# Attention outputs computed with v stationary, two heads on TensorE's two column halves, in a fused four-layer block

## What is computed

```python
# per head, 64 wide; 16 heads in a and b, 8 in h; k and v are shared by groups of heads
s = q @ k.T * scale + mask            # 256 x 256, causal: three 128x128 tiles are computed
p = exp(s - max)                      # in a, the sink joins the maximum and the denominator
o = (p @ v) / (p.sum(-1) [+ exp(sink - max)])
o = o * silu(z)                       # in a and b only: the gate
h = h + concat(o) @ w_out
# h: every key counts mult = [d<=128] + [d%4==0] + [d%16==0] times (three dilated patterns)
```

## Time and profile before

| | |
|---|---|
| median of 3 runs | 895.84 us (895.56 to 895.88) |
| the profiled execution | 895.39 us, its span 893.6 us |
| granted TensorE clock | 0.998 of full speed |
| TensorE matmul | 881.1 us busy (99%), 4570 instructions |
| TensorE weight loads | 725.3 us (81%) |
| VectorE | 557.4 us (62%) |
| ScalarE | 515.0 us (58%) |
| GpSimd | 132.6 us (15%) |
| DMA | 146.36 MB, 164 GB/s on average |

### The profile page before, as it was taken

How to read it: one execution, slowest core, us unless ns; L and a number is a source line. 1 busy time by engine, 2 the same in 40 slices (tenths; PEclk the granted TensorE clock), 3 DMA queues, 4 the chain that set the end, 5 groups by cost and what they waited for, 6 DMA issues and landing times. The chain is left out here.

```text
span 893.6 us, 12331 instructions
## 1 busy us (share of the span) xinstructions
PE 881.1 (99%) x4570; PEld 725.3 (81%) x4570; DVE 557.4 (62%) x982; ACT 515.0 (58%) x849; POOL 132.6 (15%) x104
## 2 busy tenths in 40 slices
PE   8999999999999999999999999999999999999996
PEld 5888887888878878888888887888878888888885
DVE  5855876548766677755555446566677755555444
ACT  5677566774768765644444334768765644444332
POOL 0122144121053430000000000143420000000001
PEclk9999999999999999999999999999999999999999
DMA  8732454425443334665555555544335665555521
GB/s 294 285 100 82 164 192 142 142 95 161 167 160 113 135 115 149 209 216 182 181 180 185 191 188 182 170 142 141 101 136 154 207 205 189 187 186 182 192 101 47
DMA packets 94750, 146.36 MB, mean 164 GB/s; under 512 B 6500, under 2 KB 54884, under 8 KB 94692
## 3 DMA queue, kind: packets, MB, share of 16 engines
q1 hardware_dynamic: 92804, 139.52, 46.8%
q0 software_dynamic: 1296, 4.72, 1.6%
q10 hardware_dynamic: 592, 1.34, 0.5%
HBM read 144.52 MB, written 1.05 MB: 163 GB/s over the span
## 5 line engine op out<-in xcount | busy, mean ns | idle before, releaser
L985 DVE TENSOR_TENSOR lo<-raw,hi 128x1024 fp32r<-128x1024 f32 (+1 forms) x244 | 301.3, 1260 | 132.5 <-ACT hi L1284 130.4
L1284 ACT ACTIVATE hi<-raw 128x1024 fp32r<-128x1024 f32 (+1 forms) x260 | 266.7, 1056 | 79.2 <-PE bank L1125 77.1
L1125 PE MATMUL bank<-hi,xT_hi 128*128 128x512 f32 (+2 forms) x736 | 291.8, 397 | 2.3 <-DVE xT_lo L1732 0.7
L1125 PE MATMUL bank<-hi,xT_lo 128*128 128x512 f32 (+2 forms) x736 | 283.0, 385 | 0.0
L1125 PE MATMUL bank<-lo,xT_hi 128*128 128x512 f32 (+2 forms) x736 | 282.1, 383 | 0.0
L1125 PEld LDWEIGHTS bank<-hi,xT_hi 128*128 128x128 f32 x736 | 138.4, 188 | 35.7 <-issue 8.7
L1125 PEld LDWEIGHTS bank<-hi,xT_lo 128*128 128x128 f32 x736 | 138.2, 188 | 28.2
L1125 PEld LDWEIGHTS bank<-lo,xT_hi 128*128 128x128 f32 x736 | 138.6, 188 | 24.8 <-issue 0.5
L1125 PE MATMUL bank<-hi,hT 128*128 128x512 f32 x352 | 111.5, 395 | 0.0
L1125 PEld LDWEIGHTS bank<-hi,hT 128*128 128x128 f32 x352 | 66.3, 188 | 15.4
L1125 PE MATMUL bank<-lo,hT 128*128 128x512 f32 x176 | 69.4, 394 | 0.0
(11 more groups left out here) (243 smaller groups left out, 1027.6 us busy)
## 6 DMA issues: line engine op xcount, KB each, us to landing
raw<-in_w_in SPq DMA_DIRECT2D x26, 1024.0 KB, 5.0
raw<-in_w_gate SPq DMA_DIRECT2D x44, 512.0 KB, 3.7
raw<-in_w_up SPq DMA_DIRECT2D x44, 512.0 KB, 4.7
raw<-in_w_down SPq DMA_DIRECT2D x22, 1024.0 KB, 4.8
raw<-in_w_out SPq DMA_DIRECT2D x20, 1024.0 KB, 5.0
raw<-in_w_in_b SPq DMA_DIRECT2D x10, 1024.0 KB, 5.1
raw<-in_w_in_a SPq DMA_DIRECT2D x8, 1024.0 KB, 7.1
raw<-in_w_in_a SPq DMA_DIRECT2D x4, 256.0 KB, 5.1
```

Source lines behind the costliest of these rows:

```text
L985: return engine.tensor_tensor(lo[r][:, cols], raw[c.i % RAW][:, cols], hi[r][:, cols].bitcast(F32), ALU.subtract)
L1125: last = nc.tensor.matmul(bank[:, 0:wd], still[a], mv[r][:, off:off + wd], start=c.first and i == 0 and j == 0, stop=c.last and i == len(t ...
L1284: nc.scalar.activation(hi[c.i % SPLIT][:, cols], raw[c.i % RAW][:, cols], ACT.Copy)\
```

## The change

- `v1` becomes `v`, 64 wide, without ones. In `pv`, v is stationary and probT moves: head 0 of the pair goes to the lower 64 columns of the array and of PSUM, head 1 to the upper 64, both into one bank, with 256 and then 128 moving columns for each. The outputs come out transposed, `o` is now [128, pairs, 256].
- The flips' copies to probT are all by VectorE. One pv step now handles both heads and signals once. A copy of a flip waits for the pv of the pair before it.
- In a round the order becomes: flips of pair n-1, pv of pair n-2, scores of pair n. The banks are asked for as F0, F1, V, S0, S1.
- The exponentials write their sums beside (`accum_out`) to `totals`, and `den` takes these. In h, `mult` moves into the exponent: `log_mult`, in float32, is added where the mask was.
- `gate` is now one GpSimd operation (silu(z) times reciprocals, or in h a copy of the reciprocals). It, not the output, is transposed (`turn_gate`); VectorE multiplies the bank with `o` in place, and `split_o` splits `o` into hi (ScalarE) and lo (VectorE) of oT. The gates of the second half are filled before the output product instead of after its first half chunk.

The core of the diff:

```diff
@@ attention(sc, n)
-    if 2 <= n <= pairs + 1:
-        a["obank"] = sc.bank()
-        for head in (2 * n - 4, 2 * n - 3):
-            s = sc.step("pv", head=head, att=a, bank=a["obank"], p=a["base"] + head)
-            a["pv"].append(s)
-        by_vector = (n == 4) if a["kind"] != "h" else n in (3, 5)
-        o = sc.step("vector_oev" if by_vector else "oev", att=a, pair=head // 2, bank=a["obank"], pv=s)
     if 1 <= n <= pairs:
         for head in (2 * n - 2, 2 * n - 1):
             b = sc.bank()
-            s = sc.step("flip", head=head, att=a, bank=b, p=a["base"] + head,
-                        n=len(a["flip"]) + (sc.mult_flips if a["kind"] == "h" else sc.plain_flips))
-            b.freed = (s, "vector" if a["kind"] == "h" else "scalar")
+            s = sc.step("flip", head=head, att=a, bank=b, p=a["base"] + head)
+            b.freed = (s, "vector")
             a["flip"].append(s)
+    if 2 <= n <= pairs + 1:
+        b = sc.bank()
+        s = sc.step("pv", pair=n - 2, att=a, bank=b, p=a["base"] + 2 * n - 4)
+        o = sc.step("oev", att=a, pair=n - 2, bank=b, pv=s)
+        b.freed = (o, "scalar")
@@ turn_gates(sc, a, half, *ms)
     for m in ms or range(M):
-        sc.oturned[half, m] = sc.turn(a["gates"][half][m], "o", 4 * half, m)
+        b = sc.bank()
+        s = sc.step("turn_gate", att=a, half=half, m=m, of=a["gates"][half][m], oev=a["oev"][4 * half + 3], bank=b)
+        b.freed = (s, "vector")
+        sc.turned_quarter(s)
+        sc.oturned[half, m] = sc.step("split_o", att=a, half=half, m=m, of=s)
@@ mixer_ab
+    fill_gates(sc, a, 1, zb)
     out_product(sc, w_out, KD, {
-        0: (att(9), [lambda: fill_gates(sc, a, 1, zb)]),
+        0: (att(9), ()),
@@ TensorE, pv
+                ended(pe, a["flip"][2 * s.pair + 1], "vector")
+                bank, v = freed(pe, s.bank), B["v"]
+                for r in range(2):
+                    nc.tensor.matmul(bank[64 * r:64 * r + 64, 0:S], v[:, 0, kv, :], B[f"probT{r}"][:, 0:S],
+                                     start=True, stop=False)
+                for r in range(2):
+                    last = nc.tensor.matmul(bank[64 * r:64 * r + 64, P:S], v[:, 1, kv, :], B[f"probT{r}"][:, S:QC],
+                                            start=False, stop=True)
+                last.then_inc(sem["pv", "tensor"], 1)
@@ ScalarE, scores
-                nc.scalar.activation(pr[:, 0:P], bank[:, 0:P], ACT.Exp, scale=-1.0, bias=shift[:, hd, 0:1])
+                nc.scalar.activation(pr[:, 0:P], bank[:, 0:P], ACT.Exp, scale=-1.0, bias=shift[:, hd, 0:1],
+                                     accum_out=totals[:, hd, 0:1])
                 done(nc.scalar.activation(pr[:, P:QC], bank[:, P:QC], ACT.Exp, scale=-1.0,
-                                          bias=shift[:, hd, 1:2]), s)
+                                          bias=shift[:, hd, 1:2], accum_out=totals[:, hd, 1:2]), s)
@@ VectorE
-            elif s.kind == "flip" and s.att["kind"] == "h":
+            elif s.kind == "flip":
                 dve.wait_ge(sem["flip", "tensor"], s.i + 1)
                 if s.i >= 2:
-                    dve.wait_ge(sem["pv", "tensor"], s.i - 1)
-                done(tt(Hb[f"probT{s.p % 2}"][:, :], psum[4 + s.bank.at][:, 0:QC], mult, ALU.mult), s)
+                    dve.wait_ge(sem["pv", "tensor"], s.i // 2)
+                done(nc.vector.tensor_copy(B[f"probT{s.p % 2}"][:, :], psum[4 + s.bank.at][:, 0:QC]), s)
+            elif s.kind == "turn_gate":
+                dve.wait_ge(sem["turn_gate", "tensor"], s.i + 1)
+                ended(dve, s.oev, "scalar")
+                o = B["o"][:, 4 * s.half:4 * s.half + 4, s.m * P:(s.m + 1) * P]
+                done(tt(o, psum[4 + s.bank.at][:, :].rearrange("p (k t) -> p k t", k=4), o, ALU.mult), s)
+            elif s.kind == "split_o":
+                ended(dve, s, "scalar")
+                done(tt(oT[1][:, ks, ms], B["o"][:, ks, ms], oT[0][:, ks, ms].bitcast(F32), ALU.subtract), s)
```

More of the change, by code:

```diff
@@ L431, in fill_gates @@
     es = a["sinks"][half] if a["kind"] == "a" else None
-    den = sc.step("den", att=a, half=half, es=es, oev=a["oev"][4 * half + 3])
-    a["gates"][half] = [sc.quarter("gate" if half and not m else "pool_gate", att=a, half=half, m=m, z=z, den=den) for m in range(M)]
+    den = sc.step("den", att=a, half=half, es=es)
+    a["gates"][half] = [sc.quarter("gate", att=a, half=half, m=m, z=z, den=den) for m in range(M)]
 def turn_gates(sc, a, half, *ms):
     for m in ms or range(M):
-        sc.oturned[half, m] = sc.turn(a["gates"][half][m], "o", 4 * half, m)
+        b = sc.bank()
[3 more added lines that the diff above has]
+        sc.oturned[half, m] = sc.step("split_o", att=a, half=half, m=m, of=s)
 def new_attention(sc, which, heads, nkv):
-    if sc.heads:
-        count_flips(sc)
-    a = sc.att = {"kind": which, "heads": heads, "nkv": nkv, "scores": [], "flip": [], "pv": [], "oev": [],
+    a = sc.att = {"kind": which, "heads": heads, "nkv": nkv, "scores": [], "flip": [], "oev": [],
                   "base": sc.heads, "tk": [], "tq": [], "gates": {}, "sinks": []}
@@ L956, in freed @@
             step, who = bank.before.freed
-            if step.kind == "flip":
-                eng.wait_ge(sem["flip", who], step.n + 1)
-            else:
-                ended(eng, step, who)
+            ended(eng, step, who)
         return psum[4 + bank.at]
@@ L1191, in _ @@
             elif s.kind == "pv":
[L1192 removed]
+                a = s.att
                 B = Hb if a["kind"] == "h" else A
[L1194 to L1203 removed]
+                kv = 2 * s.pair // (a["heads"] // a["nkv"])
+                ended(pe, a["flip"][2 * s.pair + 1], "vector")
[8 more added lines that the diff above has]
+            elif s.kind == "turn_gate":
+                ended(pe, s.of, "gpsimd")
+                bank = freed(pe, s.bank)
+                for i in range(4):
+                    last = transpose(bank[:, i * P:(i + 1) * P], quarter[s.of.buf][:, i * P:(i + 1) * P])
+                last.then_inc(sem["turn_gate", "tensor"], 1)
             elif s.kind == "sums":
@@ L1439, in _ @@
                 ended(act, s.pv, "tensor")
-                W1 = HD + 1
-                src = psum[4 + s.bank.at][:, 0:4 * W1].rearrange("p (g m d) -> p m g d", g=2, m=2)
-                done(nc.scalar.activation(B["o"][:, :, 2 * s.pair:2 * s.pair + 2, :], src, ACT.Copy), s)
+                done(nc.scalar.activation(B["o"][:, s.pair, :], psum[4 + s.bank.at][:, 0:S], ACT.Copy), s)
+            elif s.kind == "split_o":
+                B = Hb if s.att["kind"] == "h" else A
+                ended(act, s.of, "vector")
+                ks, ms = slice(4 * s.half, 4 * s.half + 4), slice(s.m * P, (s.m + 1) * P)
+                done(nc.scalar.activation(oT[0][:, ks, ms], B["o"][:, ks, ms], ACT.Copy), s)
             elif s.kind == "sink":
@@ L1564, in _ @@
                 last.then_inc(sem["pool_rope", "gpsimd"], 1)
-            if s.kind == "pool_gate":
-                B = Hb if s.att["kind"] == "h" else A
+            if s.kind == "gate":
                 if s.before is not None:
@@ L1821, in _ @@
                 done(tt(esink[:, e, :], shift[:, e, :], spread(sinks[:, 0, e].unsqueeze(2), [P, 8, M]), ALU.add), s)
-            elif s.kind == "vector_oev":
-                B = Hb if s.att["kind"] == "h" else A
-                ended(dve, s.pv, "tensor")
-                W1 = HD + 1
-                src = psum[4 + s.bank.at][:, 0:4 * W1].rearrange("p (g m d) -> p m g d", g=2, m=2)
-                done(nc.vector.tensor_copy(B["o"][:, :, 2 * s.pair:2 * s.pair + 2, :], src), s)
             elif s.kind == "den":
-                B = Hb if s.att["kind"] == "h" else A
-                ended(dve, s.oev, PARTS[s.oev.kind][0])
-                d = B["o"][:, :, 8 * s.half:8 * s.half + 8, HD]
+                ended(dve, s.att["scores"][8 * s.half + 7], "scalar")
@@ L1832, in _ @@
+                d = totals[:, 8 * s.half:8 * s.half + 8, :]
                 if s.es is not None:
                     ended(dve, s.es, "scalar")
-                    e = esink[:, 8 * s.half:8 * s.half + 8, :].rearrange("p s m -> p m s")
-                    chained(tt(dens[:, :, :], d, e, ALU.add))
+                    chained(tt(dens[:, :, :], d, esink[:, 8 * s.half:8 * s.half + 8, :], ALU.add))
                     d = dens[:, :, :]
                 done(nc.vector.reciprocal(dens[:, :, :], d), s)
-            elif s.kind == "gate":
+            elif s.kind == "turn_gate":
```

105 lines of the change are left out of this document (37 added, 68 removed).

## The result

| | before | after |
|---|---|---|
| median | 895.83 us (895.36 to 895.88) | 914.52 us (913.77 to 914.91) |
| ratio | | 1.0209, 95% interval 1.0194 to 1.0224 |
| span of the profiled execution | 893.6 us | 912.9 us |

The account below looks back on a forecast made before the run. TensorE, issuing without a gap, was taken to bound the kernel. Each mixer loses 2.7 + 4.0 + 1.5 - 0.2 = 8.0, two 16.0, hybrids 0: 895.4 + 16.0 = 911.4 profiled, so 911.8 median; range 903 to 921.

Parts of the forecast that it names:

- pv 0.8 from its first matmul: pv of a head pair on TensorE's column halves: 0.8 us instead of 1.29, between bounds of 0.72 and 1.4.
- The ring: Four PSUM banks: scores wait for VectorE's copy of F0, itself behind pv; TensorE's shortest round becomes 6.0 us.
- The chain through the splits: Plain rounds: exponentials, hi split, lo split, copy, scores in series set a period of 6.50 us against 5.77.
- Round 2: Mixers a and b: flips' copies delay VectorE's maxima, so scores end at 54.7 instead of 51.95, a loss of 2.7.
- The output product's start: After round 7 of a mixer: VectorE's multiplication now precedes the hi and lo splits; a loss of 1.5 us.
- Mixer a's second half of the output product: Second gates filled earlier get a half chunk more time; TensorE waits for none of it, cost 0.
- Hybrid rounds: Hybrid layers: rounds 2 and 3 lose 0.35 each, rounds 4 and 5 gain 0.4 each; together nothing.
- What costs nothing: VectorE's 32 new copies, GpSimd's single gate, earlier second gates, memset, mask transfer, read-outs in h: TensorE waits for none.
- The clock, rival at 0.03: TensorE's clock falls in gaps of 0.5 to 2.5 us; a few half chunks make 920 and more; chance 0.03.
- The second rival: Only pv, copy, scores in series binds: rounds 4 to 7 take 6.0 each, total 906.2 us; chance 0.17.
- The third: Rival: pv's two column halves don't run together, so pv costs 1.4 and the total is 919.8 us; chance 0.15.
- the first: Rival: F0's copy is in time and TensorE keeps its pace, 24 pairs gain 0.43, total 888.5 us; chance 0.08.

Follow-up runs that it names:

- the padded one: The changed kernel with 640 unused bytes a partition ahead of hT, so hT lies where the kernel before has it; 918.61 us, ratio 1.0260.

## Why the prediction was right, point by point

- **That TensorE bounds and any delay of it lengthens the kernel** held: span less busy time grew from 12.5 to 37.5 us while TensorE's own work fell by 6, and the earlier trace rows has become a list.
- **pv 0.8 from its first matmul:** 0.80 from start to start where the flips follow it, 0.87 to the end of its last instructions, and 1.5 to that end for one half after the other. Between the bounds of 0.72 and 1.4, as placed.
- **The ring**, scores behind F0's copy behind pv: 12 and 4 waits, 17.4 us, at the line named. The two kernels with other bank or step orders moved the wait to ScalarE's copy and brought plain rounds to 5.9 and 5.4.
- **The chain through the splits, 6.5 a plain round:** 6.33. The term that was too large is the read-outs' 0.4. From the first exponential to the hi split it is 1.61 now (82.15 to 83.76) and was 1.30, so 0.31 for four; the hi split starts at 2.54 and not at 2.67, and the copy follows 0.2 earlier than worked out. Without read-outs a round gains only 0.16, as the series, 6.17 where 6.0 was worked out, binds then. Over rounds 3 to 7 of a the loss is 3.4 instead of 4.0.
- **Round 2, 2.7:** 2.0. The way was right, one size was off: round 1's lo split, which stands ahead of the copies and the maxima, took 1.55 and not the 1.86 of the earlier trace rows (it starts 0.3 later beside GpSimd's rope; that this is the reason is not shown), and the read-outs took less. That copies ahead of the maxima make most of it was shown by giving them to ScalarE: 0.4 left with all of them moved, and 0.9 gained in each second round with only round 1's two moved, in the kernel with pv first.
- **The output product's start, 1.5:** 1.3 in a and 1.2 in b. The sum itself was loose: its three handoffs went in with 0.15 together, and by the text's own 0.1 each the term is 1.65. The way was partly another. pv of pair 6 got the bank that the first gate's multiplication held and waited 1.1 (the third line of the waits), which the text had not listed. Round 9 gained 0.35, predicted 0.2.
- **Mixer a's second half of the output product, 0:** 1.6. The edit that fills the second gates earlier was costed at nothing; VectorE's multiplication and lo come behind three lo splits beside GpSimd's gates, and the second tile's oT lo is 1.0 late. In b nothing is lost: the same three splits begin 1.6 us ahead of the half chunk's start that they stand beside (214.43 against 216.03), in a 0.1 behind it (101.20 against 101.08), and only a has the sinks' exponential ahead of them. No run tests that this is the reason. "I use a's values for b, whose list is the same" was wrong here: b has no sinks.
- **Hybrid rounds, 0:** 0.3 and 0.2, with 0.6 and 0.4 lost in rounds 2 and 3 and 0.3 and 0.4 gained in 4 and 5.
- **"What costs nothing" was the wrong step.** It listed copies, gates, memset and read-outs, but not the new shape of turning and splitting: a chain of six operations over two engines in strict order. It costs 4.8 us in the two scans besides the clock, and grouping four steps took all but 0.8 of it away. The earlier trace rows had the terms (0.59 and 0.68 each), and the output product's start was worked out with them; the same sum was not made for the hybrid layers, where ScalarE's next work was what counted.
- **The clock, rival at 0.03:** it was no alternative but an addition, 2.3 us in the profiled execution, and with a mean granted clock of 0.992 to 0.995 none of the five executions was free of it. That it would take "gaps, each of 0.5 to 2.5" was right; "a few half chunks, 920 and more" was not.
- **The addresses, not thought of:** -2.7. With the clock's 2.3 it nearly cancels, so the range would have been met without either.

The second rival, only the series pv, copy, scores binds, 906.2, was near: a round of 6.17 without read-outs against 6.33. The third is excluded by 0.87, the first by the waits.

The Trainium skill's "TensorEngine Tiling (Array Packing)", PSUM Bottleneck, says that once tiling has sped TensorE up, the copies out of PSUM may become the bottleneck. Its direction agrees: what the scores wait for is such a copy. But the copy's own 0.5 us is not the limit: with the flips' copies still on VectorE, another order, and a few of the output copies handed back to VectorE, 897.2 was reached.

## What to carry to other kernels

When steps are reordered, redo the ring of buffers by hand: who gets whose bank, who frees it, and what stands ahead of that on the freeing engine, in every round that differs and not only in the plain one. When one operation on each of two tiles becomes a chain across two in-order engines, issue it stage by stage and not tile by tile, and ask what the engine does next. And before a gain of 0.3% is credited to a change, put the large buffers at equal addresses in both kernels.

## What the runs showed of the hardware

- A shift of 640 bytes a partition in SBUF of the operand that 528 matmuls read changes each from 395 to 390 ns and the kernel by 2.9 us, with the same instructions and their other operand (hi, lo) where it was. The Trainium skill ("SBUF — State Buffer", SBUF: two separate sides) says, of contention between engines, that TensorE never waits on anyone. No run here shows whether the 5 ns are a wait; they come with the address of hT, and no run shows by which rule.
- TensorE's granted clock fell to its 1.2 GHz level behind gaps of 1.8 to 2.2 us at the scores, and also behind waits of 0.9 and 0.5 among short matmuls. It fell at different places in kernels with almost the same gaps (the changed kernel at 660 us, the padded one not; the kernel with pv first behind its waits in round 4, not behind those of 2 us in the hybrids), and cost 1.6 and 2.3 us where it could be set apart. So the gain of closing a gap can be more than the gap, and varies.
- A sum read out behind an exponential takes 0.19 to 0.21 us in the timeline, but four of them moved the next operation by 0.31 in all, 0.08 each.
